# Expert gates scattered into a cleared table, and the second expert sweep with token weights standing

## The reference, cut to what matters

```python
q = (ht @ w_q).reshape(T, 8, 2, 128)
s = jnp.einsum('thpd,hpkd->thpk', q, sub_keys)          # 2 x 128 sub-keys per head
top_s, top_i = lax.top_k(s, 16)
cand = top_s[:, :, 0, :, None] + top_s[:, :, 1, None, :]
cand_idx = top_i[:, :, 0, :, None] * 128 + top_i[:, :, 1, None, :]
best_s, best_c = lax.top_k(cand.reshape(T, 8, 256), 16)
expert_idx = take_along_axis(cand_idx.reshape(T, 8, 256), best_c, axis=-1)
gates = softmax(best_s)
u = expert_u[expert_idx]; act = gelu(einsum('td,thkd->thk', x, u))
out = einsum('thk,thkd->td', gates * act, expert_v[expert_idx])
```

## Time and profile before

| | us |
|---|---|
| median of 3 runs | 2929.51 (2922.83 to 2947.39) |
| profiled execution | 2924.77 |
| its span, first to last instruction | 2923.0 |
| first sweep, in the span | 988.8 to 1734.3 |
| second sweep | 1734.3 to 2272.2 |

### The profile page before, as it was taken

How to read it: one execution, slowest core, us unless ns; L and a number is a source line. 1 busy time by engine, 2 the same in 40 slices (tenths; PEclk the granted TensorE clock), 3 DMA queues, 4 the chain that set the end, 5 groups by cost and what they waited for, 6 DMA issues and landing times.

```text
span 2923.0 us, 39887 instructions
## 1 busy us (share of the span) xinstructions
PE 2869.8 (98%) x13614; PEld 2413.6 (83%) x13614; DVE 1801.1 (62%) x2935; ACT 812.5 (28%) x1351; POOL 2012.3 (69%) x1095
## 2 busy tenths in 40 slices
PE   7999999999999999999999999999999998999998
PEld 6788877788888888888888889999999765778886
DVE  5578664322125578898884027888887767776611
ACT  3244323321011212212221123333333555222201
POOL 6843574477777688998998775665652651678876
PEclk9999999999999999999999999999999998999999
DMA  4533443355664245545555469999996310223332
GB/s 162 186 116 101 141 168 115 115 187 197 219 202 158 93 138 189 191 142 180 187 189 196 140 235 381 371 348 368 350 363 224 90 62 17 73 87 100 93 94 72
DMA packets 269838, 514.79 MB, mean 176 GB/s; under 512 B 120992, under 2 KB 137504, under 8 KB 268704
## 3 DMA queue, kind: packets, MB, share of 16 engines
q1 hardware_dynamic: 226608, 382.02, 40.1%
q0 software_dynamic: 22528, 67.19, 5.9%
q10 hardware_dynamic: 20592, 64.23, 5.7%
HBM read 452.55 MB, written 127.93 MB: 199 GB/s over the span
## 4 chain that ended last, share of the span: by engine, by line
PE 92%; DVE 4%; POOL 1%; ACT 1%; issue 1%; DMA 0%; POOLq 0%; SPq 0%; ACTq 0%; DVEq 0%
PE bank L695 21%; PE bank L697 21%; PE bank L696 21%; PE banks L695 5%; PE banks L696 5%; PE banks L697 5%; PE banks L846 2%; PE banks L995 2%; PE banks L808 2%; PE banks L810 1%; PE banks L809 1%; PE banks L911 1%; PE bank L872 1%; PE banks L902 1%; POOL w_lo L564 1%
## 5 line engine op out<-in xcount | busy, mean ns | idle before, releaser
L562 POOL TENSOR_TENSOR w_hi<-w_raw,ones 128x1024 fp32r<-128x1024 f32 x364 | 697.3, 1916 | 664.2 <-PE bank L697 438.0
L564 POOL TENSOR_TENSOR w_lo<-w_raw,w_hi 128x1024 fp32r<-128x1024 f32 x364 | 893.7, 2455 | 28.6
L695 PE MATMUL bank<-h_hi,w_hi 128*128 128x512 f32 x2000 | 791.8, 396 | 8.1 <-DVE h_lo L2007 7.1
L697 PE MATMUL bank<-h_hi,w_lo 128*128 128x512 f32 x2000 | 779.6, 390 | 0.0
L696 PE MATMUL bank<-h_lo,w_hi 128*128 128x512 f32 x2000 | 778.4, 389 | 0.0
L695 PEld LDWEIGHTS bank<-h_hi,w_hi 128*128 128x128 f32 x2000 | 375.9, 188 | 92.3 <-DVE h_lo L2007 13.9
L697 PEld LDWEIGHTS bank<-h_hi,w_lo 128*128 128x128 f32 x2000 | 375.3, 188 | 79.9
L696 PEld LDWEIGHTS bank<-h_lo,w_hi 128*128 128x128 f32 x2000 | 375.9, 188 | 75.3 <-issue 2.2
L611 POOL DMA_INDIRECT v_rows<-values,v_row_of_choice x128 | 151.6, 1185 | 142.5 <-DVE token_sums L2539 112.7
L1657 ACT ACTIVATE act_out_stage<-bank 128x512 f32<-128x512 f32 x128 | 76.6, 598 | 578.3 <-PE bank L697 511.4
L619 POOL DMA_INDIRECT row_acts<-acts,act_of_choice x128 | 155.1, 1212 | 46.6 <-issue 38.4
(11 more groups left out here) (480 smaller groups left out, 5576.8 us busy)
## 6 DMA issues: line engine op xcount, KB each, us to landing
w_raw<-weights SPq DMA_DIRECT2D x430, 512.0 KB, 3.7
values<-weights SPq DMA_DIRECT2D x128, 512.0 KB, 5.0
acts<-act_out_stage ACTq DMA_DIRECT2D x128, 256.0 KB, 2.9
v_raw<-weights SPq DMA_DIRECT2D x64, 512.0 KB, 6.4
gates<-gate_stage ACTq DMA_DIRECT2D x6, 4096.0 KB, 12.9
acts_in<-acts SPq DMA_DIRECT2D x128, 192.0 KB
gates_in<-gates SPq DMA_DIRECT2D x128, 192.0 KB
resid<-x SPq DMA_DIRECT2D x4, 512.0 KB, 7.9
```

Of the source, the lines that this page charges most:

```text
L562: nc.gpsimd.tensor_tensor(w_hi[:, pair, :], w_raw[:, slot, :], one_col.to_broadcast((P, 1024)), ALU.mult).then_inc(hi_split, 1)
L564: nc.gpsimd.tensor_tensor(w_lo[:, pair, :], w_raw[:, slot, :], f32(w_hi[:, pair, :]), ALU.subtract).then_inc(split_done, 1)
L695: mm(out_, hi, rhs_hi, start=first, stop=False)
L697: return mm(out_, lo, rhs_hi, start=False, stop=last)
```

## The change

Two things are done together.

1. *Gates.* `gates` becomes a DRAM tensor of 128 x 128 keys x 384 tokens. SyncE clears it with 64 DMAs from a tile of zeros, one behind each of 64 early weight loads. For each of the three token blocks VectorE compares every choice with every other choice of its token (`merge_equal`, 16 parts of three operations), so that choices of the same expert all carry the sum of their gates, and computes the row in the table (`place_rows`). GpSimd writes them with 128 indirect DMAs per block, one four-byte word per token each (`add_gates`), and waits for completion after every 16. The one-hot path, its turns and its stage are removed. TensorE's first sweep is 128 plain tiles. Their weights are split by ScalarE (`tile_hi`) and VectorE (`tile_lo`) into four slot pairs, no longer by GpSimd. VectorE does one `tile_lo` and one part of the choices per tile, 30 tiles per token block.
2. *Second sweep.* The token weights (128 tokens) stand in TensorE, and 512 value features move: 3 blocks x 2 halves x 3 = 18 matmuls of 512 columns per key, into six banks (tokens in partitions). After the last key VectorE and ScalarE copy the six banks to `dense`, and TensorE turns them, 24 blocks, together with the 8 of `summed` (`turn_dense`). `sweep_added` then waits for each of the eight banks.

Several SBUF addresses move with this, and `ret_gate` (VectorE) waits for the clearing, since the zeros lie where a later tensor is put.

```diff
+DENSE_BANK = ((2, 3, 0), (5, 6, 7))
...
+            clear = n - CLEAR_FROM
+            if clear == 0:
+                sp.wait_ge(consts_set, 3)
+            if 0 <= clear < CLEARS:
+                some = NKEYS // CLEARS
+                sp.dma_start(gates[clear * some:clear * some + some, :, :].rearrange("e k t -> k e t"),
+                             zeros[:].unsqueeze(1).to_broadcast((P, some, DT))).then_inc(gates_cleared, 16)
...
-                sp.dma_start(g_in[:, slot, :].rearrange("p (b t) -> p b t", t=STAGED_TOKENS),
-                             gates[:, :, bass.ds(key, 1), :].rearrange("b k a t -> k b (a t)")).then_inc(key_in[u], 16)
+                sp.dma_start(g_in[:, slot, :], gates[bass.ds(key, 1), :, :].rearrange("a k t -> (a k) t")).then_inc(key_in[u], 16)
...
-        sp.wait_ge(gates_out, c.due(gates_out, 16 * DB * LOTS))
+        for n in range(DB):
+            sp.wait_ge(gates_added[n], 16 * CHOICES)
...
+        def add_gates(n):
+
+            for j in range(CHOICES):
+                if j % PART == 0:
+                    pool.wait_ge(rows_ready, n * MERGE_PARTS + j // PART + 1)
+                if j and j % TOPK == 0:
+                    pool.wait_ge(gates_added[n], 16 * j)
+                pool.indirect_dma_start(
+                    out=gate_words, out_offset=bass.IndirectOffsetOnAxis(ap=gate_at[:, n, j:j + 1], axis=0),
+                    in_=gate_of[:, n, j:j + 1], in_offset=None).then_inc(gates_added[n], 16)
+
+        pool.wait_ge(gates_cleared, 16 * CLEARS)
+        for n in range(DB):
+            add_gates(n)
...
+        def first_layer(i):
+            for n in range(RAW):
+                hi, lo = value_slot(n)
+                pe.wait_ge(acc_read_act, c.due(acc_read_act, 1, back=2))
+                pe.wait_ge(split_done, c.due(split_done))
+                for k in range(KT):
+                    col = slice(k * P, (k + 1) * P)
+                    ins = three(bank[n % 2][:], hi[:, col], lo[:, col], h_hi[:, k, :], h_lo[:, k, :], k == 0, k == KT - 1)
+                ins.then_inc(tile_done, 1)
+        c.repeat(NKEYS // RAW, first_layer)
...
-                        for m in range(4):
-                            if first and q == half == e == 0 and m == 1:
-                                pe.wait_ge(acc_read_act, c.due(acc_read_act, 0))
-                            col = slice(e * 512 + m * P, e * 512 + m * P + P)
-                            ins = three(bank[half * 4 + m][:, 0:DT], hi[:, col], lo[:, col],
-                                        ew_hi[:, q * 2 + e, 0:DT], ew_lo[:, q * 2 + e, 0:DT],
+                        key, col = q * 2 + e, slice(e * 512, e * 512 + 512)
+                        for tt in range(DB):
+                            tok = slice(tt * P, tt * P + P)
+                            ins = three(bank[DENSE_BANK[half][tt]][:], ew_hi[:, key, tok], ew_lo[:, key, tok], hi[:, col], lo[:, col],
                                         first and q == 0 and e == 0, ends and e == 1)
...
+        def turn_dense():
+
+            pe.wait_ge(acc_read_act, c.due(acc_read_act, 0))
+            pe.wait_ge(row_summed, CHOICES)
+            pe.wait_ge(dense_by_dve, DB)
+            for k in range(KT):
+                if k == 4:
+                    pe.wait_ge(dense_by_act, DB)
+                for tt in range(DB):
+                    ins = nc.tensor.transpose(bank[k][:, tt * P:tt * P + P], dense[:, tt, k * P:k * P + P], t_("identity"))
+                    if k == tt == 0:
+                        ins.then_inc(tile_done, 1)
+                turn_sums(k).then_inc(bank_summed, 1)
...
+        def tile_hi(n):
+
+            at = START["experts"] + n
+            act.wait_ge(raw_loaded[n % RAW], 16 * (at // RAW + 1))
+            act.wait_ge(tile_done, at - RAW + 1)
+            fn(value_slot(n)[0], w_raw[:, n % RAW, :], ACT.Copy).then_inc(v_hi_ready, 1)
...
+        for key in range(NKEYS - 2):
+            if key + 3 < NKEYS:
+                tile_hi(key + 3)
+            key_act(key, key % 2)
+            if key % CHOICE_TILES == SHARES_AT and key // CHOICE_TILES < TT:
+                shares()
...
+        dve.wait_ge(gates_cleared, 16 * CLEARS)
         c.repeat(RET_HEADS, ret_gate)
...
+            tt_(pairs, chosen[:, 2, own].unsqueeze(2).to_broadcast(big), chosen[:, 2, :].unsqueeze(1).to_broadcast(big), ALU.is_equal).then_inc(dve_step, 1)
             dve.wait_ge(dve_step, c.due(dve_step))
+            tt_(pairs, pairs, chosen[:, 3, :].unsqueeze(1).to_broadcast(big), ALU.mult).then_inc(dve_step, 1)
+            dve.wait_ge(dve_step, c.due(dve_step))
+            ve.tensor_reduce(gate_of[:, tt, own], pairs, AX.X, ALU.add).then_inc(rows_ready, 1)
...
+        for n in range(2, NKEYS):
+            tile_lo(n)
+            if n < TT * CHOICE_TILES:
+                choices(n // CHOICE_TILES, n % CHOICE_TILES)
...
+        for tt in range(DB):
+            ve.tensor_copy(dense[:, tt, 0:512], bank[DENSE_BANK[0][tt]][:]).then_inc(dense_by_dve, 1)
```

More of the change, by code:

```diff
@@ L52 @@
 COPY_FROM = 8
+CLEARS = 64
+CLEAR_FROM = 10
 PAIR_SLOTS = 4
@@ L309, in build @@
     bank += [nc.alloc_psum_tensor(f"bank{n}", [P, T], F32) for n in range(6, 8)]
[L310 to L313 removed]
+    gates = nc.dram_tensor("gates", (NKEYS, NKEYS, DT), F32, kind="Internal").ap()
     values = nc.dram_tensor("values", (NKEYS, P, 2, 512), F32, kind="Internal").ap()
@@ L670, in _ @@
         c.repeat((N_STREAM - START["up"]) // RAW, four)
-        splits((N_STREAM - START["up"]) % RAW)
+        for s in range((N_STREAM - START["up"]) % RAW):
+            split(s)
         for j in range(0, KT, 2):
@@ L999, in _ @@
-        tiles_fm(TURN_AT, h_hi, h_lo, acc_read_act)
-        pe.wait_ge(score_read, c.due(score_read, 0))
-        turn(0)
-        tiles_fm(LEAD_TILES - TURN_AT, h_hi, h_lo, acc_read_act)
-        def mixed(n, first, next_choices=0):
-            gate_batches()
-            for k in range(n):
-                p = (first + k) % 2
-                pe.wait_ge(acc_read_act, c.due(acc_read_act, 1, back=2))
-                tile_fm(p, h_hi, h_lo, bank[p][:])
-                if k == 0 and next_choices:
-                    turn(next_choices)
@@ L2505, in weigh_key @@
+        count_tokens()
+        dve.wait_ge(split_done, START["experts"])
+        for n in range(2):
+            tile_lo(n)
+        for part in range(2):
+            choices(0, part)
+        for n in range(2, NKEYS):
+            tile_lo(n)
+            if n < TT * CHOICE_TILES:
+                choices(n // CHOICE_TILES, n % CHOICE_TILES)
         def weigh_key(key):
```

309 lines of the change are left out of this document (94 added, 215 removed).

## The result

The change made the kernel slower: 3010.8 us (median of 4 executions, 2976.3 to 3036.1) against 2929.3 us before (2922.8 to 2947.4). Two of the four, the profiled one among them (3022.0 us, span 3020.2), are over 1.5% above the fastest and count as slow; the other two (2976.3 and 2999.6) give the ratio of 1.020, with a 95% interval of 1.017 to 1.024. So it is slower beyond doubt, while whether by more than 2% is open. The forecast was 2866.

A forecast was written before the change was run, and what follows sets the result against it. TensorE, busy 98% of the span, was taken as the bound; -49.2 - 15.6 + 5.5 = -59.3 us on 2924.8 gave 2865.5, stated as 2866. The range reached from smaller term 3 and cheaper second sweep to a scatter some 55 us late.

The forecast's parts named there:

- Term 1: First sweep, TensorE: one-hot matmuls, turnings and seams go, leaving 696.3 of 745.5 us: -49.2 us if nothing new stalls TensorE.
- VectorE's budget: First sweep: VectorE's choosing, subtractions and merges take 156 of 163 us per 30 tiles; cost 0, bounds 0 and +15 us.
- The scatter on GpSimd: First sweep: 384 indirect DMAs at 1.36 us, done at 1646 us, 30 us early; cost 0, bounds 0 and +130.
- Clearing: Gate table cleared by 64 DMAs of 384 KB from tile 10 on: cost 0, bounds 0 and +3 us.
- Term 2: Second sweep: 18 matmuls of 512 columns per key replace 24 of 384, 522.3 us: -15.6 us, bounds -19 and 0.
- Term 3: Between second sweep and next stage: dense sums must be copied and turned, +5.5 us, bounds +3 and +9.
- B: Rival: scatters at 1.51 us each end at 1703 us, late by 27: 2893 us; chance 0.24.
- C: Rival: scatters take 1.51 us and completions 7.5, so TensorE stands 127 us: 2993 us; chance 0.09.
- D: Rival: GpSimd's indirect DMAs hold up VectorE, merge tiles take 8.7 us instead of 5.44: 3009 us; chance 0.04.
- E: Rival: second sweep gains nothing because operand supply, not matmul count, sets its pace: 2881 us; chance 0.05.

The follow-up runs named there:

- x1_none: The changed kernel without its 384 scatters, so the gates never reach the table: 2889.2 us (before 2944.9).
- z2_ceiling: The changed kernel without scatters, with aligned operand addresses and the second sweep's first gathers spread: 2863.3 us (before 2926.4).
- z1_halves: The changed kernel with aligned addresses, spread gathers and scatters paced at 1.7 per half tile: 2877.5 us (before 2926.4); over four executions 2882.0, ratio 0.981.
- y4_second: The kernel before with only the change's second-sweep part, one-hot matmuls and old gates kept: 2925.9 us (before 2940.6).
- y1_align: x3_paced with the v slots and high and low weighted activations moved to multiples of 1 KB: 2889.8 us (before 2940.6).
- x3_paced: The changed kernel with GpSimd waiting for TensorE's tiles, seven scatters per two tiles: 2909.7 us (before 2944.9).
- x2_reads: The changed kernel with each scatter replaced by a four-byte gather at the same indices: 3089.4 us (before 2944.9).
- x4_sixteen: The changed kernel with each scatter carrying 16 partitions instead of 128, same number of DMAs: 3204.2 us (before 2944.9).
- y3_three: The changed kernel with aligned addresses, spread gathers and scatters paced at three per tile: 2944.9 us (before 2940.6).

## Why the prediction was wrong

The profiled execution is 3022.0 - 2865.5 = 156.5 us over the forecast. The runs place nearly all of it: 132.6 stalls in the first sweep (after against x1_none); 705.6 - 696.5 = 9.1 the v slots' addresses; 1152 x (0.2335 - 0.2267) = 7.8 the w slots' in the second sweep; and the rest of the second sweep, 538.7 - 522.2 - 7.8 = 8.7, gaps and lower clock behind its first gathers. That is 158.2, 1.7 more than 156.5; z2_ceiling, with none of the four, lies 2.2 under the forecast. The first item is that of one execution: over the four, 2976.3 to 3036.1, the excess over the forecast runs from 111 to 171 us, and no trace of a shorter one was kept.

**Term 1, first sweep, -49.2.** Right as worked out (z2_ceiling: 745.5 - 696.5 = 49.0), and it had its condition with it: "if nothing new stalls TensorE".

**VectorE's budget.** Right: the three operations of a merge part took 1.22, 1.23 and 1.22 us, subtractions 1.23, and no idle of TensorE for weight halves where scatters are absent. Cost 0 stands.

**The scatter on GpSimd: the step that failed.** It was put at cost 0, priced only by when it ends. Its pace (1.36 us from start to start forecast, 1.27 in the median measured), its completion (3 us forecast, 2 measured) and its end (1646 forecast, the last start was 1676.0, after 53 us of waiting for merges behind the first scatter) were near enough, and z1_halves puts lateness at 6 us. What issuing them does to the other engines was given no term and no bound, and in place of nothing it took 132.6 us. The upper bound of +130 us, worked out for lateness, comes near that by luck. The trace of before had shown such DMAs only where GpSimd was held up between them, at most 57 in 100 us (8 in the densest 10), where after has 71. A resource used at a pace that the trace doesn't show should have got a bound of its own.

**Clearing.** Right, no cost: the first sweep starts at 988.6 us in after, 988.8 before.

**Term 2, second sweep, -15.6.** Mis-sized: in after +0.8, of which 7.8 us are addresses and 8.7 gaps and clock; in y4_second, without the gaps, -5; with aligned operands and spread gathers 522.2 - 537.9 = -15.7. "The pitch of 0.2267 us stands" was read from a duration (389 ns at L808), and from matmuls of w with h, which do lie at the same offset. Start-to-start times of v and w in the second sweep before (0.1734 and 0.1759) would have shown that the slots differ.

**Term 3, the seam, +5.5.** From the sweep's last matmuls to the span's end it was 2923.0 - 2272.2 = 650.8 us before and 2861.5 - 2207.2 = 654.3 in z2_ceiling: +3.5, within its bounds.

**Rivals.** B and C priced lateness. In after the sweep itself ended later than the scatters, so nothing was late; in z1_halves lateness cost 6 us. The waits for the four-byte writes, some 2 us, did not go toward the 7.5 us of C. D (VectorE held up by GpSimd) came out at 3009 us, close to the result, which is luck: its mechanism is refuted, since VectorE's 128x1024 operations stay at 1.22 to 1.23 us in the mean under 384 scatters. By the Trainium skill (SBUF — State Buffer, SBUF: two separate sides) the loser of the shared port would block; here only GpSimd does. VectorE's idle time in the sweep was mostly a wait for ScalarE's halves (132.5 and 92.1 us), as ScalarE waited for TensorE. E (second sweep gains nothing, by operand supply), with chance 0.05, came true in after by its number; operand supply, which y1_align shows to be a matter of address, is about half of it, the gaps are the rest.

The forecast's mechanism for the gain was right and is worth 63 us (2926.4 to 2863.3) when nothing is scattered, the operands are aligned and the first gathers spread; with the scatters paced as well, 60 of 2942 us remain. Without the new addresses some 17 of them would go.

## What to carry to other kernels

Give GpSimd's indirect DMAs a pace when something else must run beside them: here 6 per 10 us (65 in the densest 100 us), tied to a semaphore of the bound engine, and check that the last one still meets its deadline. A price for work moved to an idle engine needs a second line, what its issue does to the others; the sign of it in a trace is idle time by issue in the middle of an accumulation. Let both operands of a matmul begin at the same offset within 512 bytes, and read the pace from start to start, not from a duration.

## What the hardware did that was not expected

- Where GpSimd started 71 or more indirect DMAs within 100 us, TensorE started a matmul only every 0.7 to 1.4 us for stretches at a time, waiting for nothing that the profile shows. VectorE had such gaps too (3.83 us at 1198.34 us), and the DMA engines moved 51 GB/s from 1140 to 1250 us instead of 144 (z1_halves). How much of what VectorE, ScalarE and the DMA engines lost is their own, and how much is waiting for TensorE's tiles, is not separated.
- A single row of 16 did nothing: 16 started in 20.4 us from 1109.1 in after, and in 20.7 us from 1383.7 in x3_paced, without a gap. Twenty in 25 us, with no pause behind the sixteenth, brought gaps at the start of the second sweep of x3_paced, the first some 20 us after the row began. The first gap came at 1151 us in after, in the fourth row of 14 to 16 scatters, at 1154 in x2_reads, in the third, and at 1089 in x4_sixteen, in the second. At 5.5 per 10 us (y3_three) there was no gap, at 67 in 110 us (z1_halves, from 1140) none, at 75 in the same 110 us (after) TensorE stood for over a third of the time.
- Neither direction nor number of words mattered. Where in the chip this happens no run tells. One rival is untested: each execution on record lists a span and a granted clock, that is, it was traced, so no run shows the gaps without the writing of these records. And records were lost: of the 16 completion records that each DMA leaves, the trace of before has 20590 of 20640, that of after 16703 of 27712. Against it, x1_none has no gap in the first sweep and lost records too (16727 of 21568).
- The granted clock fell behind the gaps (full to 1156 us, then 0.50; 0.70 in the mean from 1140 to 1250 us, in which TensorE idled for over a third), so that 84 us of idle cost 133.
- An indirect DMA of 16 partitions took GpSimd 0.92 us, one of 128 partitions 1.06: nearly all of the cost is per instruction.
- A scatter was seen complete some 2 us after its instruction ended on GpSimd, 3 us after it began. The Trainium skill (DMA: Bandwidth & Descriptors, Anatomy of one DMA — SWDGE (gpsimd) path) gives about 2.0 us of fixed cost, setup and completion, for a DMA issued by GpSimd; the trace agrees if one counts from the end of the instruction.
- Matmuls of 512 columns run at 0.2267 us where both operands have the same offset within 512 bytes, and at 0.2324 to 0.2338 where they lie 128 bytes apart.
